# Layer 0 experts: four result buffers in place of two, with a store loop of four pieces per turn

## The reference

```
for l in range(2):
    h  = modulate(rms(x), ...);  hc = modulate(rms(xc), ...)
    x  = x + g1 * (attention(h, hc) @ w_out[l])        # and xc in layer 0
    tokens = [modulate(rms(x)); modulate(rms(xc))]      # 512 rows in layer 0
    gates  = top 2 of 16 experts for each token, weights that sum to 1
    for e in range(16):
        he = silu(tokens @ w_gate[e]) * (tokens @ w_up[e])
        y += gates[:, e] * (he @ w_down[e])
    x = x + g2 * y                                      # and xc in layer 0
```

## Time and profile before

| | us |
|---|---|
| median of 3 runs | 1113.79 |
| lowest, highest | 1113.63, 1115.46 |
| the profiled execution | 1113.13 |
| its span in the trace | 1111.4 |

### The profile page before, as it was taken

One profiled execution on the slowest core, in us unless ns is written; L12 is line 12 of the kernel. 1 busy time (PEld: TensorE's weight loads), 2 busy tenths in 40 slices (PEclk: granted clock), 3 DMA queues, 4 the chain that ended last, 5 costly groups with the idle time before them and its releaser, 6 DMA issues. The chain is left out here.

```text
span 1111.4 us, 24577 instructions
## 1 busy us (share of the span) xinstructions
PE 940.3 (85%) x9667; PEld 583.0 (52%) x9668; DVE 483.1 (43%) x1365; ACT 299.0 (27%) x678; POOL 44.6 (4%) x65
## 2 busy tenths in 40 slices
PE   5699989898996979999988926998988786766997
PEld 2244655443444846666655615786567553433554
DVE  1446656567124633333333317576833441222343
ACT  3322245455003411011010115226723120111111
POOL 0000000000000001011111130000000000000000
PEclk9899999999896899999999968999997998888999
DMA  8994079698503009999999986006033399999961
GB/s 321 429 385 144 1 314 415 252 358 354 223 0 152 1 10 391 415 418 420 366 417 420 417 323 251 0 3 245 1 152 152 118 429 427 428 429 428 429 259 38
DMA packets 33040, 298.25 MB, mean 268 GB/s; under 512 B 9008, under 2 KB 10432, under 8 KB 16096
## 3 DMA queue, kind: packets, MB, share of 16 engines
q1 hardware_dynamic: 23264, 286.14, 62.7%
q0 software_dynamic: 8016, 11.21, 3.1%
q10 hardware_dynamic: 1712, 0.23, 0.1%
HBM read 289.51 MB, written 15.86 MB: 275 GB/s over the span
## 5 line engine op out<-in xcount | busy, mean ns | idle before, releaser
L716 PE MATMUL bank<-ring,rows_buf 128*32 128x256 f32 x4160 | 254.4, 399 | 60.7 <-DMA ring<-in_w_up_dram 35.1
L716 PEld LDWEIGHTS bank<-ring,rows_buf 128*32 128x32 f32 x4160 | 159.5, 115 | 148.8 <-issue 83.8
L728 PE MATMUL bank<-ring,rows_buf 128*32 128x256 f32 x2080 | 127.0, 383 | 11.6 <-ACT work L993 11.5
L489 PE MATMUL bank<-rows_buf,ring 128*128 128x512 f32 (+1 forms) x320 | 117.8, 523 | 12.5 <-ACT rows_buf L883 6.5
L728 PEld LDWEIGHTS bank<-ring,rows_buf 128*32 128x32 f32 x2080 | 71.7, 110 | 57.8 <-issue 28.2
L489 PEld LDWEIGHTS bank<-rows_buf,ring 128*128 128x128 f32 x320 | 62.4, 196 | 60.7 <-issue 47.1
L1404 DVE COPY rows_buf<-rows_buf x176 | 52.3, 297 | 87.3 <-DVE rows_buf L1404 45.8
L589 PE MATMUL bank<-rows_buf,ring 128*128 128x512 f32 (+1 forms) x256 | 85.5, 497 | 1.0 <-DVE rows_buf L1204 1.0
L1160 DVE RECIPROCAL work<-work 128x512 f32<-128x512 f32 (+1 forms) x20 | 54.3, 2713 | 59.3 <-ACT work L893 59.3
L1182 DVE TENSOR_REDUCE rows_buf<-bank 128x1 f32<-128x512 f32 (+1 forms) x96 | 57.4, 598 | 44.7 <-PE bank L530 22.9
L589 PEld LDWEIGHTS bank<-rows_buf,ring 128*128 128x128 f32 x256 | 49.5, 194 | 37.5 <-issue 31.5
(11 more groups left out here) (215 smaller groups left out, 1044.6 us busy)
## 6 DMA issues: line engine op xcount, KB each, us to landing
ring<-in_w_gate_dram SPq DMA_DIRECT2D x32, 2048.0 KB, 14.8
ring<-in_w_up_dram SPq DMA_DIRECT2D x32, 2048.0 KB, 19.5
ring<-in_w_down_dram SPq DMA_DIRECT2D x32, 2048.0 KB, 17.0
ring<-in_ada_w_dram SPq DMA_DIRECT2D x24, 2048.0 KB, 10.5
ring<-in_w_in_dram SPq DMA_DIRECT2D x8, 1536.0 KB, 23.2
y_rows<-in_table_dram SPq DMA_DIRECT2D x1, 8704.0 KB, 58.4
ring<-in_w_out_dram SPq DMA_DIRECT2D x4, 2048.0 KB, 10.3
y_rows<-work POOLq DMA_DIRECT2D x42, 128.0 KB, 10.5
```

Of the source, the lines that this page charges most:

```text
L489: last = mm(bank[1 + i % 2][:, 0:widths[i]], qk_weights(i, k), h_t[:, k, 0:widths[i]], start=(k == 0), stop=(k == KD - 1))
L716: last = mm(o.rearrange("r (s c i) -> r s c i", s=2, c=KF), hc_t[l][:, k, :], w[:, :, k, :, CHUNK * q:CHUNK * q + CHUNK], start=(k == 0), ...
L728: last = mm(bank[4][CHUNK * q:CHUNK * q + CHUNK, 0:256], he_t[l][:, k, :], wd[:, k, 256 * q:256 * q + 256], start=(k == 0), stop=(k == KF ...
```

## The change

Four result buffers of 256 columns each stand side by side in `work` in place of two. One scratch tile, `act_g`, moves by 8 columns to make room. There are four semaphores `rows_stored`. `row_out(g)` waits for the store of piece g-4 and for nothing younger. The store loop takes four pieces a turn: (42 + 3) // 4 = 11 turns, which is 44 stores, where (42 + 1) // 2 = 21 turns made 42. The two additional stores come last, send whatever is in their buffers, and write to rows that no token uses. ScalarE's last increment of `rows_ready` is 3. The zero stores at the start follow the number of buffers: 4 + 3 = 7 in place of 2 + 1 = 3.

```diff
-        y_out0 = [work[:, 512 + 512 * i:768 + 512 * i] for i in range(2)]
+        y_out0 = [work[:, 264 + 256 * i:520 + 256 * i] for i in range(4)]
...
-        rows_stored = [sem(f"rows_stored{i}") for i in range(2)]
+        rows_stored = [sem(f"rows_stored{i}") for i in range(4)]
...
                 def row_out(g):
                     act.wait_ge(down_mm[l], g + 2)
-                    act.wait_ge(rows_stored[0], (g + 2) // 2 * 16)
-                    act.wait_ge(rows_stored[1], (g + 3) // 2 * 16)
-                    nc.scalar.copy(work[:, bass.ds(g % 2 * 512 + 512, 256)], bank[4][:, 0:256]).then_inc(rows_ready, 1)
+                    act.wait_ge(rows_stored[0], (g + 4) // 4 * 16)
+                    act.wait_ge(rows_stored[1], (g + 7) // 4 * 16)
+                    act.wait_ge(rows_stored[2], (g + 6) // 4 * 16)
+                    act.wait_ge(rows_stored[3], (g + 5) // 4 * 16)
+                    nc.scalar.copy(work[:, bass.ds(g % 4 * 256 + 264, 256)], bank[4][:, 0:256]).then_inc(rows_ready, 1)
...
                     act.wait_ge(rows_ready, total + 1)
-                    act.sem_inc(rows_ready, 1)
+                    act.sem_inc(rows_ready, 3)
...
                 if l == 0:
                     act.wait_ge(rows_stored[0], 16)
-                    act.wait_ge(rows_stored[1], 32)
+                    for i in range(1, 4):
+                        act.wait_ge(rows_stored[i], 32)
                 qkv(l)
...
             for turns in (1, 2):
-                for i in range(turns - 1, 2):
+                for i in range(turns - 1, 4):
                     pool.dma_start(y_rows[ROWS:ROWS + CHUNK, :].rearrange("r (q c) -> q r c", q=4),
                                    ring[:, 8, 0:256]).then_inc(rows_stored[i], 16)
                     pool.wait_ge(rows_stored[i], 16 * turns)
...
-                with pool.Fori(0, (total + 1) // 2) as m:
-                    for i in range(2):
-                        pool.wait_ge(rows_ready, 2 * m + i + 2)
-                        pool.dma_start(y_rows[bass.ds(2 * CHUNK * m + CHUNK * i, CHUNK), :].rearrange("r (q c) -> q r c", q=4),
+                with pool.Fori(0, (total + 3) // 4) as m:
+                    for i in range(4):
+                        pool.wait_ge(rows_ready, 4 * m + i + 2)
+                        pool.dma_start(y_rows[bass.ds(4 * CHUNK * m + CHUNK * i, CHUNK), :].rearrange("r (q c) -> q r c", q=4),
                                        y_out0[i]).then_inc(rows_stored[i], 16)
                 pool.wait_ge(pos_ready, l + 1)
-                pool.wait_ge(rows_stored[0], (total + 3) // 2 * 16)
-                pool.wait_ge(rows_stored[1], (total + 5) // 2 * 16)
+                pool.wait_ge(rows_stored[0], (total + 7) // 4 * 16)
+                for i in range(1, 4):
+                    pool.wait_ge(rows_stored[i], (total + 11) // 4 * 16)
```

More of the change, by code:

```diff
@@ L210, in backbone @@
         hc_t = [a.rearrange("p (k r) -> p k r", k=KD) for a in hc_flat]
-        act_g = [work[:, 1280:1408], hflat[:, 1024:1152]]
+        act_g = [work[:, 1288:1416], hflat[:, 1024:1152]]
         he = [spare[:, 0:128], hflat[:, 1152:1280]]
```

## The result

| | before | after |
|---|---|---|
| median, us (20 runs each) | 1114.83 | 1119.44 |
| lowest, highest | 1110.72, 1119.74 | 1114.73, 1125.40 |
| profiled execution | 1113.13 | 1121.86 |
| span in the trace | 1111.4 | 1119.8 |

The ratio after to before is 1.0042, 95% interval 1.0024 to 1.0060: slower by 2.7 to 6.7 us. A second series, beside the last experiments, gave 1.0055 (1.0032 to 1.0077). The forecast was +4.9 us.

What follows compares the result with a forecast made beforehand. Full DMA engines and TensorE were taken to end layer 0's expert phase nearly together. 1113.13 + 5.1 (stall) + 1.9 (clock) - 2.1 (tail) = 1118.0; the profiled execution lies 0.66 under the median, giving 1118.7 us, range 1111.5 to 1125.5.

Steps and rivals of the forecast that it cites:

- The zero stores: Start, on GpSimd: seven chained stores, the added four 10.4 us each beside full DMA engines, last landing at 66 us.
- the discount of 2 us: Start: taken off the 68.1 us last landing, because stores taking turns with the shorter packets of `w_in` land sooner.
- The stall: Start, layer 0's `qkv(0)`: TensorE waits 5.1 us for ScalarE's result; bounds 0 and 18 us.
- The clock: Start, behind TensorE's new gap: it falls to half clock, costing 1.9 us more.
- No taking up later: After the start: TensorE's projections run without a gap, so nothing gives the 5.1 us back; later phases begin later.
- TensorE's waits in the phase: Layer 0 expert phase: 13 waits for the copy, 8.5 us, go; TensorE then waits about 1 us for weights, costing nothing.
- The tail: End of layer 0's expert phase: the last three stores land with the last loads, near 651.5 us plus 0.4; gain 2.1 us.
- Rival 1: Start: added zero stores land in 4.0 us each, no stall, only the 2.1 us gain remains, 1111.7 us; chance 8%.
- Rival 2: Layer 0 expert phase: gives back TensorE's waits in full, 11.5 us; with the stall 1109.3 us; chance 5%.
- rival 3: Start and tail: zero stores of 9.3 us, stall 2.6, clock 1.3, tail gain 4.5; 1113.2 us, no difference; chance 12%.
- The two start terms: Start: TensorE's 5.1 us wait ahead of L477 and 1.9 us of half clock behind it, 7.0 us.
- the phase's gain: Layer 0 expert phase: gathers 2.1 us earlier, as the last stores land with the last loads; bounds 4.5 gain, 9 loss.

## Why the prediction was right

Forecast 1118.7, measured 1119.44, in absolute terms a closeness of luck, since the median of before moved by 1 us with more runs; the change, +4.9 forecast, is +4.7 by the ratio. The steps:

- *The zero stores.* Right: place, chain, releaser. Forecast 10.4 us each less 2 for `w_in`, last landing 66; the three issue gaps were 11.2, 10.0 and 11.3 us, 32.5 against 3 x 10.7 = 32.1, and ScalarE started at 68.66. Without the discount of 2 us the forecast would have been 68.1: the discount was the error, a shorter gap shows at one store only (46.74 - 36.72). The stall was 6.7 to 6.9 us, forecast 5.1.
- *The clock.* 1.9 forecast, 2.5 in the two-buffer run with seven stores, 2.8 after. The 1.9 was read from one trace, behind the 6.48 us gap ahead of the first 32 matmuls. Over the fourteen kernels that same gap was followed by 15.86 to 16.79 us for them, against 14.06 at full clock: 1.8 to 2.7 us. The value taken was near the lower end of a scatter that one trace could not show.
- *No taking up later.* Right: from the second L477 to GpSimd's first copy behind the projections it is 71.1 us before and after. And the changed kernel with 128-row and with 16-row zero stores differs by 1.0055 - 0.9967, 0.9% or 9.8 us: what the start lost is still there at the end.
- *TensorE's waits in the phase.* Right that they go (11.5 to 1.2), right that the DMA queue is late next. Mis-sized, though off the path of the end: TensorE waits 7.7 us for weights, not 1. I let the weights land 2.6 us earlier for the closed hole. From first refill to the landing of expert 15's up matrix it was 209.2 us before (625.2 - 416.0) and, issued at 603.79, 603.79 + 30.9 - 426.22 = 208.5 after: 0.7 us.
- *The tail.* 2.1 us forecast, by three last stores that land with the last load. So it was: `w_out` lands at 642.22 + 18.7 = 660.9, 234.7 us after the first refill where it was 236.4 (1.7 earlier, forecast 1.5 to 3.5), and the gather follows at 662.48. From refill to gather the two-buffer kernels took 238.9, 238.1 and 239.1, the four-buffer ones 236.3, 236.0, 235.8, 235.4, 235.8 and 235.3: a gain of 2.9 us, one trace each. From the first expert matmul it is 259.1 to 259.7 and 256.1 to 257.5, a gain of 2.3.
- *Rival 1* (quick stores) is out, and with it, for a store beside a full queue, the fit of the Trainium skill (DMA: Bandwidth & Descriptors, Anatomy of one DMA, SWDGE path), by which 2.3 us was the estimate: it took 10.5, and the measurement decides. *Rival 2* (the full 11.5 us back) is out too. Its observation, that no row shows TensorE waiting for weights, was true and proved nothing: the wait comes to light when the other is taken away.

In the prediction's rival 3, four stores of 9.3 us end at 25.3 + 4 x 9.6 = 63.7 and not at 63.5, which changes nothing.

The two start terms were 2.4 to 3.0 us too small together (7.0 forecast, 9.4 in the two-buffer run, 10.0 after), the phase's gain 0.2 to 0.8 too small. The errors partly cancel. The steps as measured add up to about 7 us, the two traces alone differ by 8.4, the ratios say 4.7 and 6.1. So the mechanism and the sign were right, and that the forecast of 4.9 came within a few tenths of the first ratio is luck.

## What to carry to other kernels

When buffers are added, count everything that is done once per buffer: here setup stores in a chain, each as long as a store takes beside full queues, ran over the slack of an engine 50 us later and cost over three times the gain. Before removing a wait, look what else is as late as it is. If two resources end together, the removed wait comes back under another name. For setup DMAs on GpSimd issue them side by side, or small, or when the DMA engines are quiet.

## What the runs showed of the hardware

- A GpSimd store beside full DMA engines landed in 5.6 us with 32 packets and in 10.1 and 10.5 us with 144 and 141, though 144 carried half the bytes of 141. The second zero store of 128 rows, beside a DMA share of 0.68 (10.6 to 14.8 us, before), took 3.6 to 4.1 us over the runs.
- TensorE's clock: behind gaps of 6.7 to 6.9 us the next stretch between two L477 was 2.5 to 2.8 us longer, behind one of 5.5 us (zero stores of 64 rows, 68.03 to 77.74) 1.5 us.
- Runs of one kernel scatter by up to 9 us (1110.72 to 1119.74 of before), more than the net change of 4.7. The traces differ in stretches that no change touched: from GpSimd's first copy behind the projections to the first expert matmul it took 250.7 to 255.6 us over the fourteen kernels, from layer 1's first projection to its first expert 186.9 to 189.0.
- 8 indirect gathers took 5.7 us to landing alone and 18.9 us beside 6 MB of loads.
